# The final sums of a streaming encoder step: sample tile first, last prompt tile in column halves

## What is computed

```python
    a = jax.nn.silu(g) * u * comb[..., None].astype(h.dtype)
    routed = jnp.einsum('tef,efd->td', a, p['w_down'])
    shared = (jax.nn.silu(h @ p['w_sg']) * (h @ p['w_su'])) @ p['w_sd']
    return routed + shared
...
    x = x + g2[:, None] * lax.map(lambda hs: moe_ffn(hs, p), h2)
...
    y_prompt = rms(xp) * g_final
    y_sample = rms(xs) * g_final
```

## Time and profile before

| what | value |
|---|---|
| median of 3 runs | 1203.01 us (1200.45 to 1206.89) |
| the profiled execution's own time | 1195.38 us |
| its span, first to last instruction | 1193.6 us |
| busy share of the span | PE 93%, DVE 30%, ACT 24%, POOL 24% |
| mean granted TensorE clock | 0.974 of full speed |

### The profile page before, as it was taken

One profiled execution on the slowest core, in us unless ns is written; L12 is line 12 of the kernel. 1 busy time (PEld: TensorE's weight loads), 2 busy tenths in 40 slices (PEclk: granted clock), 3 DMA queues, 4 the chain that ended last, 5 costly groups with the idle time before them and its releaser, 6 DMA issues.

```text
span 1193.6 us, 19520 instructions
## 1 busy us (share of the span) xinstructions
PE 1104.4 (93%) x6631; PEld 695.7 (58%) x6632; DVE 358.8 (30%) x918; ACT 283.0 (24%) x738; POOL 291.6 (24%) x494
## 2 busy tenths in 40 slices
PE   4999999898999899699999989989999999999994
PEld 1775676454666644466666646646666665666541
DVE  3100000284454323552222222222222222222447
ACT  3200100286565201301111111111111111111232
POOL 1000100102222100043443433333434433443300
PEclk9999999999898999899999999999999999999998
DMA  8822412222543000647989999998998999999295
GB/s 345 309 71 70 150 71 71 80 71 87 184 164 131 1 1 16 275 179 271 376 329 376 415 414 415 415 415 363 379 350 345 400 413 414 412 391 389 83 410 144
DMA packets 77649, 304.26 MB, mean 255 GB/s; under 512 B 13302, under 2 KB 15416, under 8 KB 59496
## 3 DMA queue, kind: packets, MB, share of 16 engines
q1 hardware_dynamic: 60696, 268.26, 57.5%
q0 software_dynamic: 16256, 33.08, 7.4%
q10 hardware_dynamic: 656, 2.36, 0.5%
HBM read 290.26 MB, written 33.82 MB: 272 GB/s over the span
## 4 chain that ended last, share of the span: by engine, by line
PE 76%; DMA 14%; DVE 4%; ACT 2%; issue 2%; POOL 1%; SPq 1%; ACTq 0%; POOLq 0%; DVEq 0%
PE bank L992 22%; PE bank L999 12%; DMA arena<-in_w_down 9%; PE bank L665 6%; PE bank L666 6%; PE bank L735 5%; PE bank L922 5%; PE bank L985 3%; DMA arena<-y_rows 3%; PE bank L846 2%; PE bank L1004 2%; DMA arena<-in_w_ada 1%; PE bank L873 1%; PE bank L822 1%; PE bank L627 1%
## 5 line engine op out<-in xcount | busy, mean ns | idle before, releaser
L992 PE MATMUL bank<-arena 128*64 128x256 f32 x2880 | 332.6, 382 | 22.2 <-DMA arena<-in_w_down 13.8
L992 PEld LDWEIGHTS bank<-arena 128*64 128x64 f32 x2880 | 248.7, 138 | 129.8 <-issue 73.2
L999 PE MATMUL bank<-arena 128*64 128x512 f32 x728 | 176.3, 601 | 1.5 <-DVE arena L1729 0.6
L1735 DVE COPY arena<-bank 128x512 f32<-128x512 f32 x90 | 62.3, 692 | 335.5 <-PE bank L985 335.5
L1306 ACT COPY arena<-bank 128x128 f32<-128x128 f32 x90 | 23.9, 266 | 419.6 <-PE bank L1004 419.6
L545 POOL DMA_INDIRECT arena<-h_rows,arena x93 | 98.4, 1058 | 82.5 <-POOL arena L542 78.9
L553 POOL DMA_INDIRECT y_rows<-arena x91 | 93.4, 1027 | 86.2 <-POOL arena L550 81.5
L665 PE MATMUL bank<-arena 128*128 128x288 f32 x320 | 104.0, 407 | 0.3 <-DVE arena L1459 0.3
L666 PE MATMUL bank<-arena 128*128 128x288 f32 x320 | 103.8, 406 | 0.0
L1729 DVE COPY arena<-bank 128x512 f32<-128x512 f32 x91 | 62.9, 692 | 102.1 <-PE bank L999 102.1
L999 PEld LDWEIGHTS bank<-arena 128*64 128x64 f32 x728 | 52.1, 136 | 67.2 <-issue 66.4
(11 more groups left out here) (282 smaller groups left out, 1118.3 us busy)
## 6 DMA issues: line engine op xcount, KB each, us to landing
arena<-in_w_gate SPq DMA_DIRECT2D x64, 1024.0 KB, 10.9
arena<-in_w_up SPq DMA_DIRECT2D x64, 1024.0 KB, 15.0
arena<-in_w_down SPq DMA_DIRECT2D x64, 1024.0 KB, 15.8
arena<-in_w_ada SPq DMA_DIRECT2D x8, 2048.0 KB, 7.9
arena<-in_w_in SPq DMA_DIRECT2D x5, 2048.0 KB, 11.1
arena<-y_rows SPq DMA_DIRECT2D x3, 3072.0 KB, 16.7
arena<-in_w_ada SPq DMA_DIRECT2D x8, 1024.0 KB, 17.1
arena<-in_w_out SPq DMA_DIRECT2D x2, 2048.0 KB, 7.9
```

The source lines that it names most:

```text
L992: last = pe.matmul(bank[0][n * SLOT:n * SLOT + SLOT, 0:2 * P].rearrange("p (g f) -> p g f", f=P), HGT[:, k % 4, k // 4, :], w[:, :, n * P: ...
L999: last = pe.matmul(bank[3][n * SLOT:n * SLOT + SLOT, :], AE[:, f, :], DN[j][:, f, 512 * n:512 * n + 512], start=(f == 0), stop=(f == 1))
L1735: dve.tensor_copy(hgt, bank[1][:, :]).then_inc(hgt_ready, 1)
```

## The change

The order of the tiles becomes 4, 0, 1, 2, 3 (`ORDER`) on all engines, so the sample is loaded, summed and finished first. `YP` becomes a list: the last tile, now prompt tile 3, has three rows on PE, so DVE adds two weighted rows there in place of one. The last tile goes through PE in column halves: all three rows of the left half, then those of the right half, with a semaphore after each (`sd_done`). DVE (`routed_last`) sums, gates and adds each half by itself, ACT squares each half by itself, DVE adds the two sums of squares (one more column in `SS`), and the scaling and the store are in halves as well. DVE's sixth-row additions move to `own_rows`, and for the last tile `own_rows` and `finish` of the tile before it come ahead of `routed_last`. The sample now uses bank 6, which is also one of prompt tile 3's, so `shared_out(3)` waits until DVE has read the sample's sums.

```diff
-YP = 4
+YP = [4, 4, 4, 3, 4]
+ORDER = [4, 0, 1, 2, 3]
...
-        SDB = [(0, 1), (2, 3), (4, 5), (6, 7), (0, 0)]
+        SDB = [(0, 1), (2, 3), (4, 5), (6, 7), (6, 6)]
...
-            for t in range(2):
-                pe.wait_ge(g2_ready, t + 1)
-                shared_out(2 + t)
-            for t in range(NT):
-                if t == 4:
-                    pe.wait_ge(acc_ready, 1)
-                    shared_out(4)
-                routed_out(t)
+            pe.wait_ge(g2_ready, 1)
+            shared_out(2)
+            pe.wait_ge(g2_ready, 2)
+            shared_out(4)
+            routed_out(0)
+            pe.wait_ge(acc_ready, 1)
+            shared_out(3)
+            for i in range(1, NT):
+                routed_out(i)
...
+            t = ORDER[-1]
+            for n in range(2):
+                c = slice(512 * n, 512 * n + 512)
+                act.wait_ge(fin_x, NT + n)
+                ins = act.activation(y_row(t, 1)[:, c], X[:, t, c], ACT.Square, accum_out=SS[:, (t, NT)[n]:(t, NT)[n] + 1])
+            ins.then_inc(fin_sq, 1)
...
+            def routed_last():
+
+                t = ORDER[-1]
+                acc = y_row(t, YP[t])
+                for n in range(2):
+                    c = slice(512 * n, 512 * n + 512)
+                    dve.wait_ge(sd_done, NT + n)
+                    chain(dve.tensor_tensor(acc[:, c], acc[:, c], sd_out(t, n), ALU.add))
+                    chain(dve.tensor_tensor(acc[:, c], acc[:, c], G2[:, 0, c], ALU.mult))
+                    dve.tensor_tensor(X[:, t, c], X[:, t, c], acc[:, c], ALU.add).then_inc(fin_x, 1)
+
+            own_rows(0)
+            routed(0)
+            dve.wait_ge(gf_ld, 16)
+            for i in range(1, NT - 1):
+                own_rows(i)
+                routed(i)
+                finish(i - 1)
+            own_rows(NT - 1)
+            finish(NT - 2)
+            routed_last()
             finish(NT - 1)
```

More of the change, by code:

```diff
@@ L151, in build @@
         GA = at(take(2), 2)
-        SS = at(take(NT), NT)
+        SS = at(take(NT + 1), NT + 1)
         RS = at(take(NT), NT)
@@ L220, in build @@
         EJ = at(a_tmp + 4736, TOPK, NE)
-        DIAG = at(a_tmp + 2048, 2, YP, P)
+        DIAG = at(a_tmp + 2048, 2, max(YP), P)
         YB = [[(0, at(a_ring, TOPK, D))],
@@ L419, in _ @@
             sp.wait_ge(hg_staged, pairs * 2 + 2)
-            for t in range(NT):
+            for t in ORDER:
                 r = ROWS[t]
@@ L424, in _ @@
                     sp.dma_start(part[0:r], rows[:, k:k + part.shape[1], :]).then_inc(yb_ld[t], 16)
-            for t in range(NT):
-                sp.wait_ge(y_ready, t + 1)
+            for i, t in enumerate(ORDER[:-1]):
+                sp.wait_ge(y_ready, i + 1)
                 r = ROWS[t]
@@ L429, in _ @@
                 sp.dma_start(dst, X[0:r, t, :]).then_inc(y_stored, 16)
-            sp.wait_ge(y_stored, 16 * NT)
+            t = ORDER[-1]
+            for n in range(2):
+                sp.wait_ge(y_ready, NT + n)
+                sp.dma_start(y_prompt[0, t * P:t * P + P, 512 * n:512 * n + 512], X[:, t, 512 * n:512 * n + 512]).then_inc(y_stored, 16)
+            sp.wait_ge(y_stored, 16 * (NT + 1))
         @block.gpsimd
@@ L454, in _ @@
             pool.wait_ge(ms_ready, 1)
-            pool.tensor_tensor(RS, SS, HALF[:, 0, 0:NT], ALU.pow).then_inc(rs_ready, 1)
+            pool.tensor_tensor(RS, SS[:, 0:NT], HALF[:, 0, 0:NT], ALU.pow).then_inc(rs_ready, 1)
             for a, (kp_o, ks_o, vp_o, vs_o) in enumerate(((ak_p, ak_s, av_p, av_s), (bk_p, bk_s, bv_p, bv_s))):
@@ L578, in _ @@
             pool.wait_ge(gathered[1], (pairs + 1) * 16)
-            for t in range(NT):
-                pool.wait_ge(fin_ms, t + 1)
+            for i, t in enumerate(ORDER):
+                pool.wait_ge(fin_ms, i + 1)
                 pool.tensor_tensor(RS[:, t:t + 1], SS[:, t:t + 1], HALF[:, 0, 0:1], ALU.pow).then_inc(fin_rs, 1)
@@ L1057, in shared_out, with routed_out @@
                     pe.matmul(sd_out(t, n), SA[:, f, t * P:t * P + r], WSD[:, f, 512 * n:512 * n + 512], start=(f == 0), stop=False)
-            def routed_out(t):
+            def routed_out(i):
+                t = ORDER[i]
                 r = ROWS[t]
-                pe.wait_ge(diag_ready, t + 1)
+                pe.wait_ge(diag_ready, i + 1)
                 pe.wait_ge(yb_ld[t], 16 * len(YB[t]))
-                for k in range(YP):
-                    for n in range(2):
-                        last = pe.matmul(sd_out(t, n), DIAG[0:r, t % 2, k, 0:r], y_row(t, k)[:, 512 * n:512 * n + 512], start=False, stop=(k == YP - 1))
+                each = [(k, n) for n in range(2) for k in range(YP[t])] if i == NT - 1 else [(k, n) for k in range(YP[t]) for n in range(2)]
+                for k, n in each:
+                    last = pe.matmul(sd_out(t, n), DIAG[0:r, i % 2, k, 0:r], y_row(t, k)[:, 512 * n:512 * n + 512], start=False, stop=(k == YP[t] - 1))
+                    if i == NT - 1 and n == 0 and k == YP[t] - 1:
+                        last.then_inc(sd_done, 1)
                 last.then_inc(sd_done, 1)
@@ L1323, in _, with diagonals, first_term @@
             act.wait_ge(w6_ready, 1)
[L1325 to L1330, removed]
+            def diagonals(i):
+                t = ORDER[i]
+                if i >= 2:
+                    act.wait_ge(sd_done, i - 1)
+                for k in range(YP[t]):
+                    ins = act.activation(DIAG[:, i % 2, k, :], IDENT, ACT.Copy, scale=W6[:, t, k:k + 1])
                 ins.then_inc(diag_ready, 1)
-            def first_term(t):
-                acc = y_row(t, YP)
+            def first_term(i):
+                t = ORDER[i]
+                acc = y_row(t, YP[t])
                 act.wait_ge(yb_ld[t], 16 * len(YB[t]))
-                act.activation(acc, acc, ACT.Copy, scale=W6[0:ROWS[t], t, YP:YP + 1]).then_inc(yb_first, 1)
+                act.activation(acc, acc, ACT.Copy, scale=W6[0:ROWS[t], t, YP[t]:YP[t] + 1]).then_inc(yb_first, 1)
             diagonals(0)
@@ L1342, in _ @@
             first_term(1)
[L1343 to L1348, removed]
+            for i, t in enumerate(ORDER[:-1]):
+                if i + 2 < NT:
+                    diagonals(i + 2)
+                    first_term(i + 2)
+                act.wait_ge(fin_x, i + 1)
+                squares(t, y_row(t, 1) if t < 4 else YB[4][0][1][:, 1, :], fin_sq, i)
+            t = ORDER[-1]
[4 more added lines that the diff above has]
+            ins.then_inc(fin_sq, 1)
         @block.vector
@@ L1753, in _, with finish, own_rows, routed @@
             dve.sem_inc(w6_ready)
-            def finish(t):
+            def finish(i):
+                t = ORDER[i]
                 r = ROWS[t]
-                dve.wait_ge(fin_sq, t + 1)
+                dve.wait_ge(fin_sq, i + 1)
+                if i == NT - 1:
+                    chain(dve.tensor_tensor(SS[:, t:t + 1], SS[:, t:t + 1], SS[:, NT:NT + 1], ALU.add))
                 dve.tensor_scalar(SS[:, t:t + 1], SS[:, t:t + 1], 1.0 / D, EPS, ALU.mult, ALU.add).then_inc(fin_ms, 1)
-                dve.wait_ge(fin_rs, t + 1)
-                dve.scalar_tensor_tensor(out=X[0:r, t, :], in0=X[0:r, t, :], scalar=RS[0:r, t:t + 1], in1=GF[0:r, :], op0=ALU.mult, op1=ALU.mult).then_inc(y_ready, 1)
-            def routed(t):
-                r = ROWS[t]
[L1766 to L1771, removed]
+                dve.wait_ge(fin_rs, i + 1)
+                for c in [slice(0, 512), slice(512, D)] if i == NT - 1 else [slice(0, D)]:
+                    dve.scalar_tensor_tensor(out=X[0:r, t, c], in0=X[0:r, t, c], scalar=RS[0:r, t:t + 1], in1=GF[0:r, c], op0=ALU.mult, op1=ALU.mult).then_inc(y_ready, 1)
+            def own_rows(i):
+                t = ORDER[i]
+                acc = y_row(t, YP[t])
+                dve.wait_ge(yb_ld[t], 16 * len(YB[t]))
+                dve.wait_ge(yb_first, i + 1)
+                for k in range(YP[t] + 1, TOPK):
+                    chain(dve.scalar_tensor_tensor(out=acc, in0=y_row(t, k), scalar=W6[0:ROWS[t], t, k:k + 1], in1=acc, op0=ALU.mult, op1=ALU.add))
+            def routed(i):
+                t = ORDER[i]
+                r = ROWS[t]
+                acc = y_row(t, YP[t])
+                dve.wait_ge(sd_done, i + 1)
                 for n in range(2):
@@ L1775, in routed @@
                 ins.then_inc(acc_ready, 1)
-                dve.wait_ge(acc_ready, t + 1)
+                dve.wait_ge(acc_ready, i + 1)
                 dve.wait_ge(g2_ready, 2)
```

## The result

The changed kernel takes 1207.68 us in the median of 20 runs (1201.14 to 1214.10), the kernel before 1203.04 in the median of 20 (1195.35 to 1209.01). The ratio is 1.0040 with a 95% interval of 1.0022 to 1.0058: +4.6 us, and by the interval +2.6 to +7.0. That is slower, but less than the 0.5% that the prediction counted as a difference.

The account below looks back on a forecast made before the run. DVE's full queue was taken to bound the end; own rows +1.3, halves +0.4, last `finish` +1.2 and store -0.4 gave +2.5 us, bounds +0.5 to +4.5. Forecast median 1205.5 us, range 1198 to 1211.

Parts of the forecast that it names:

- rival (2): At PE's new wait before `shared_out(3)`: a late sample lowers PE's clock, +6.5 to +9 us, about 1211; 7 in 100.
- four terms: At the kernel's end: own rows +1.3, halves +0.4, last `finish` +1.2, last store -0.4, summing to +2.5 us.
- the ±0.7 of the start: Start of DVE's full queue: forecast at 1158.96 us, give or take 0.7 for when the sample lands.
- What bounds the end: On DVE from 1158.96 us: its queue is full, so the end is the sum of its entries, 29.4 us.
- DVE's queue, +2.9: DVE's queue to the last scaling: added own row +1.3, halves +0.4, last `finish` with uncovered square +1.2 us.
- The store, -0.4: Last store, now 256 KB: taken as 2.5 us, saving 0.4 us (bounds -0.8 and 0).
- DVE's full queue begins at the same moment: PE's second tile in the new order ends as before, despite a 1.4 us gap, so DVE's queue starts at 1158.96.
- a granted clock below 1.00: Sign on PE: a granted clock falling below 1.00 before 1180 us would show the forecast wrong.
- Rival (1): Tail after tile 3's landing: with DVE free then, it ends at 1186.7, 1.7 us earlier; 8 in 100.
- Rival (3): At the end: moved `finish` and halves overlap better, square fully hidden, only +0.5 to +1 us, 1203.8; 15 in 100.

Follow-up runs that it names:

- e3: The changed kernel with four rows on PE for the last tile too; 62.44 us from the first load's issue to the last instruction, against 65.04.
- e4: The changed kernel with the last tile summed, squared, scaled and stored whole, not in halves; 63.64 us from first load's issue to last instruction, against 65.04.
- e8: The changed kernel, unchanged, profiled again; 65.72 us from the first load's issue to the last instruction, against 65.04.
- e7: The changed kernel with PE's wait filled, four PE rows for the last tile, first four tiles' scaling on GpSimd and ACT; ratio to the kernel before 0.9977.

## Why the prediction was right, and what it sized wrongly

The forecast was +2.5 us, no difference that can be told at 0.5%, with bounds from +0.5 to +4.5 and a range of 1198 to 1211 us for the median; measured were 1207.68, +4.6 in the medians and +5.1 in the profiles. The class and the range held, but the size was half of what came, and it lies just outside the bounds of the sum. The range held because it took in the scatter of the runs and half of rival (2), not because the sum was right. The sum's bounds were loosely added as well: its four terms and the ±0.7 of the start give +0.8 to +4.4. Measured, the 5.1 are +2.6 of DVE's late start, +2.6 of its queue and -0.1 behind it.

- **What bounds the end: right.** DVE's queue is full from its first sums to the last scaling. e3 takes one row off it and the queue is 1.33 us shorter (30.71), though PE has more to do; e4 takes the halves away and it is 1.6 us shorter (30.46).
- **DVE's queue, +2.9: right.** Measured +2.64 (32.04 - 29.40). By terms: two own rows 2.63 (1188.75 to 1191.38) in place of 1.30, so +1.3; halves 4.18 in place of 3.81, so +0.4; the last `finish` 3.20 behind the sums, with `finish(2)` 5.21 in place of 4.07, so +1.1 (forecast +1.2). That is 2.8; the 0.2 us that DVE waited for PE before 1173.45 are gone.
- **The store, -0.4: the landing was right, the gain wasn't there.** A half is 256 KB and takes 2.0 us from issue to landing, against 2.9 for the sample. That is the floor: the prediction has it as 2.1, but 2.6 less 0.6 is 2.0. From the end of the last scaling to the last instruction it is 5.13 us (1205.9 - 1200.77), against 5.24: -0.1. By the waits of SP's queue the end now waits 1.7 us for that landing and then 2.8 for PE's queue (2.4 and 2.1 before), so the gain is given back at the end of the program. Why it is, no run here tells.
- **PE, "DVE's full queue begins at the same moment": this step failed.** It began 2.6 us later (27.87 for 25.28). The gap was as forecast (1.54 us for 1.4). What was mis-sized are two terms. From the start of `shared_out(3)` to the start of tile 0 was priced at 3.43 us and took 4.95 (1161.59 - 1156.64), because PE worked at 1.2 GHz for 2.9 us of it: +1.5. In e3, at a clock of 1.00, it takes 3.54. And PE was to start on the sample's rows where tile 0 had landed, 9.7 us after the first issue, and started at 10.59 (1151.45 - 1140.86): +0.9. The sample landed 10.3 to 10.7 us after the first issue in all kernels with the new order, against 9.8 to 9.9 for tile 0. The prediction took the distance of two landings with a full tile ahead, 7.3 us, for the time at the head of the queue, and overlooked that the second of the sample's two transfers closes it. PE had its shared parts done at 9.92 and its rows were there after 9.1; whether a wait for the first transfer alone would give the difference, no run tells.
- **Rival (2), PE's clock, at 7 in 100: its mechanism came true, at a smaller price.** The prediction named a granted clock below 1.00 as a sign that it is wrong, and that sign is there. It tied the fall to a late sample and a gap of 4 us, and took a stretch in which PE stood still for 1.5 of 5 us at a clock of 1.00 as evidence against it. That row is a sum over 48 instructions; it doesn't say that the 1.5 us were in one piece, and it says nothing of how often. One gap of 1.5 us was enough in four of five executions. The Trainium skill (TensorE: Matmul & The Clock Gate, Part 1) says that the moment of a clock change isn't fixed by the program's own work and so differs from run to run; e3 and e8, the same gap without and with a fall, agree with that. The slow multiplications cost 1.4 us here, the lower end of the 1.4 to 4 that the rival gave them; its other part, a delay of 2.5 us, wasn't there, since the sample landed only 0.7 late.
- **Rival (1), a shorter tail: fell** as argued. It needs DVE free when tile 3 lands. e7, which takes the scaling of four tiles off DVE, is what gets near: 53.85 us to the last scaling, against 54.68 before and the 1186.7 - 1133.68 = 53.0 that the rival gave.
- **Rival (3), nothing moves: fell.** The square is bare, 0.79 us of wait on DVE.

## What to carry to other kernels

Before work is cut into halves to shorten a tail, look at which engine's queue is full there: this tail was a sum of DVE's instructions, and each half, each added row and each uncovered wait was an addition to it, however early the inputs came. A gap on TensorE can be paid twice, once as the wait and once, in four of five executions here, as slow multiplications behind it; two multiplications that need nothing (here the other half of `shared_out(3)`) fill it for a few lines of code. And a difference of 5 us in a kernel whose executions differ by 14 is measured in the profile from an event just ahead of the change, not over the whole.

## What the runs showed of the hardware

**GpSimd and DVE hold each other up.** In e7 GpSimd multiplies 64x1024 elements in 2.34 us (L590; L592 is its power):

```profile
1162.40 2.34 POOL L590 TENSOR_TENSOR arena<-arena 64x1024 f32<-64x1024 f32 x1 [20.55 <-DVE arena L1830]
...
1172.77 1.55 POOL L592 TENSOR_TENSOR arena<-arena 128x1 f32<-128x1 f32 x1 [8.02 <-DVE arena L1801]
1174.31 2.34 POOL L590 TENSOR_TENSOR arena<-arena 128x1024 f32<-128x1024 f32 x1
...
1188.61 2.35 POOL L590 TENSOR_TENSOR arena<-arena 128x1024 f32<-128x1024 f32 x1
```

and DVE instructions with two SBUF inputs that start within such a multiplication (the first and the last row here) take as much longer:

```profile
1162.53 3.31 DVE L1815 SCALAR_TENSOR_TENSOR arena<-arena 128x1024 f32<-128x1024 f32 x1 [0.30 <-ACT arena L1359]
...
1172.61 1.27 DVE L1815 SCALAR_TENSOR_TENSOR arena<-arena 128x1024 f32<-128x1024 f32 x1
1175.87 1.28 DVE L1825 TENSOR_TENSOR arena<-arena,bank 128x512 f32<-128x512 f32 x2 [1.99 <-PE bank L1082]
...
1189.05 2.46 DVE L1840 TENSOR_TENSOR arena<-arena 128x512 f32<-128x512 f32 x1
```

These two take 1.28 and 0.69 us elsewhere in the same kernel (L1815 at 1186.96, L1840 at 1192.87). 1162.53 + 3.31 - 1.28 = 1164.56 is where the first would have had to start, and GpSimd's instruction ends at 1164.74; so the second engine does next to nothing until the first is through. DVE's sums, which read one input from a bank, aren't held up: L1825 takes 1.28 us at 1175.87, inside a multiplication of GpSimd from 1174.31 to 1176.65. And GpSimd waits in its turn: its power, 0.54 us alone, takes 1.55 at 1172.77, while DVE is at L1815 (1172.61, 1.27 us). e7 paid 3.8 us of DVE's time for this, 2.0 of them ahead of a wait for PE. The Trainium skill (SBUF — State Buffer, Who interferes with whom) has it that a DVE instruction with two SBUF inputs and a GpSimd instruction that reads SBUF exclude each other, the later one waiting; these rows agree.

**The clock's fall isn't decided by the program alone.** The same order with the same 1.5 us of gap gave `shared_out(3)` in 5.1 to 5.4 us in four executions, with the granted clock at 0.50 for about 3.4 us, and in 3.70 in one, at 1.00. Nor does the fall have to come in the gap: in the changed kernel's profile it came 1.0 us into it, in e4 0.7 us and in e8 1.1 us after PE was multiplying again. e4, where PE is back at 1157.28, in the view by windows:

```profile
1157.16:1157.66 0.50, 0.38 (x1) 1.00 1.60 688
1157.66:1158.16 0.50, 0.50 (x2) 0.85 0.23 98
1158.16:1158.66 0.50, 0.50 (x2) 0.50 1.73 737
```

So the price differs with the part of the slow stretch that falls on work: 5.11 us where 0.5 us of it were idle, 5.40 where none was.

**A load first on an empty queue can land later with half the bytes.** 1.5 MB into 64 partitions, in two transfers, were there 10.3 to 10.7 us after the first issue, 3 MB into 128 partitions in one transfer after 9.8 to 9.9. The first transfer alone, 1.25 MB, took 9.1 to 9.2. How much is the number of partitions and how much the second transfer, no run separates.
